# Matmuls of constants into a spare PSUM bank, issued by TensorE behind seven norms of a two-block transformer kernel

## Chip, core and metric

The kernel runs on one core of a Trainium2 chip. The metric is the device time of one launch in microseconds (us); lower is better. Before the change the median of 3 runs is 2633.58 us (2631.14 to 2635.16).

## What is computed

A sequence of 512 tokens of width 1024, all in fp32, goes through two blocks of two layers each. The first block has an mLSTM layer and a forgetting-attention layer, each followed by a gated feed-forward of width 2816 with a short convolution. The second has a layer of spatial gating and neighbourhood attention, a conformer convolution layer, and a feed-forward of width 4096 after each. The part that matters here is the norm, which stands between all the large products:

```python
def rmsnorm(x, w):
    xf = x.astype(jnp.float32)
    y = xf * lax.rsqrt(jnp.mean(xf * xf, axis=-1, keepdims=True) + EPS)
    return (y * w.astype(jnp.float32)).astype(x.dtype)

for layer in range(DEPTH):
    h = rmsnorm(x, norm_mix_pre[layer])
    y = ...
    x = x + rmsnorm(y, norm_mix_post[layer])
    h = rmsnorm(x, norm_ffn_pre[layer])
    y = conv_ffn(h, ...)
    x = x + rmsnorm(y, norm_ffn_post[layer])
```

The second block adds modulated norms of the same kind (`mlp0`, `odd`, `mlp1` below), a layer norm inside the conformer convolution (`conf`), and a last `rmsnorm_2(x, final_g)` (`final`) before the output.

## The kernel before

Activations lie with the features on the 128 partitions: `X`, `Y`, `H_hi`, `H_lo` and `hid_hi`, `hid_lo` are 8 tiles of 128 features by 512 tokens. A large product is computed as three products in a rounded fp32 format (`F32R`): each weight and each activation is split into a high and a low part, and TensorE (PE) multiplies high by high, low by high and high by low. So one product of a 128-row step is three matmuls of 512 columns (line 2277), and one group of 256 output features is 8 steps by 2 halves by 3, 48 matmuls, into a pair of banks of the PSUM tensor `G`. Stages of a few groups follow each other in the order of `linear_plan`.

ScalarE (ACT) makes the high part of each weight chunk (`split_hi`, line 497), VectorE (DVE) the low part (`split_lo`, line 502), SyncE (SP) issues the weight loads, GpSimd (POOL) loads the modulation weights. Every engine's program is written out by hand, in order; semaphores join them. Nothing reorders the work.

A norm goes like this. ACT squares 512-column tiles into `SQ` or `SA`. PE sums the squares over the features by multiplying with the 128x128 tile `ones`, in plain fp32, into bank `M[:, 0]`. ACT takes logarithm and exponential of the sum (lines 435 and 437), which gives the inverse root for each token, in `root` (the profile calls it `Dg`). DVE multiplies it in, and ACT and DVE split the result into `H_hi` and `H_lo`. Only then can PE start the next product. There are three patterns around the change:

- `post0` and `post1` (behind the stages `m_out` and `x_out`): after the sum, DVE adds the normed `Y` to `X` (lines 484 and 479), ACT squares the new `X` (line 445), and PE sums these squares tile by tile (`norm_tiles`, line 2345), in between the matmuls of the next stage (`ffn1`), one sum and six matmuls for each tile.
- `mlp0`, `odd`, `mlp1`: after the sum, DVE and ACT fill `H_hi` and `H_lo` (lines 470, 353, 365), and PE starts the next stage when the first `H_lo` tile is there. `conf` is the same with a SiLU in between (lines 2126, 2015, 2034, 2121).
- `final`: DVE writes the normed tiles to `S` (line 2140), PE transposes them (line 1971), ACT copies them out of PSUM (line 2029), and SP stores them (line 1480).

For all but `conf` the sum is issued by `squares_behind`, one matmul of `ones` with the collected squares `SA` (line 2324) and two with `SQ` (line 2327), behind the last group of a stage. For `conf` it is `norm("conf")`, eight sums (line 2345). A plain fp32 matmul stands in the profile as two weight loads and two matmuls. Bank `M[:, 2]`, the tile `ident` (a 128x128 identity) and the tile `VT` (all small vectors, turned) are there already; `M[:, 2]` holds nothing that is still to be read at the seven places.

Of the kernel before, what the change touches and what calls it, by code (L numbers as in the profile page):

```python
# [33 lines left out]
GC = 256  # L34
# [94 lines left out]
def build(nc, a, out, consts):  # L129

    plan, chunks = linear_plan()
    with ExitStack() as ctx:
# [3 lines left out]
        def at(name, offset, shape, dt=F32):  # L136
            return nc.alloc_sbuf_tensor_at(name, shape, dt, offset=origin + offset)
# [18 lines left out]
        VT = at("VT", 184 * K + 512, [P, VBLOCKS * P])  # L156
# [7 lines left out]
        def small(name, shape, dt=F32):  # L164
            n = 4
            for s in shape[1:]:
                n *= s
            t = at(name, o[0], shape, dt)
            o[0] += -(-n // 32) * 32
            return t  # L170

        ident = small("ident", [P, P])
# [78 lines left out]
        M = ctx.enter_context(nc.psum_tensor("M", [P, 4, 512], F32))  # L251
# [71 lines left out]
        def group_of(name, g):  # L323
            return plan[name]["group"] + g

        def wait_read(eng, name, g):
            n = group_of(name, g)
            eng.wait_ge(pair_read[n % 2], n // 2 + 1)
# [5 lines left out]

        first_use = lambda name, g: group_of(name, g) // 2
        used_after = lambda name: 4 + 2 * group_of(name, plan[name]["groups"])

        ident4 = ident[:].unsqueeze(1).to_broadcast([P, TB, P])

# [374 lines left out]
        def mod_sums(pe, layer):  # L714

            pe.wait_ge(mod_used, 48 * layer + 48)
            for r in range(3 if layer else 4):
                if r == 3:
                    pe.wait_ge(mod_e, 1)
                for c in range(4):  # L720
                    mm = pe.matmul(M[32 * c:32 * c + 32, 1 + r % 3, :], ones[:, 0:32], mod_source(r)[:, c * T:c * T + T],
                                   start=True, stop=True, skip_group_check=True)
                mm.then_inc(mod_p, 1)
# [7 lines left out]
        def mod_columns(pe, layer):  # L731

            count = 3 if layer else 4
            pe.wait_ge(mod_e, 4 * layer + count)
            for r in range(count):
                for q in range(4):
                    first = 16 * r + q
                    mm = pe.matmul(M[:, 3, first:first + 13:4], mod_source(r)[:, q * P:q * P + P], ident[:, 0:P:32],
                                   start=(r == 0 and q == 0), stop=(r == count - 1 and q == 3), skip_group_check=True)
            mm.then_inc(mod_s, 1)  # L740
# [742 lines left out]
        def bias_rows_pe(pe):  # L1483
            pe.wait_ge(rp_dma, 64)
            pe.transpose(M[:, 2, 0:120], rp[:], ident[0:120, 0:120]).then_inc(tb_t, 1)

        def bias_pe(pe):

            pe.wait_ge(tb_r, 8)
            wait_all_read(pe, "c_v")  # L1490
            for u in range(10):
                if u % 2 == 0:
                    pe.wait_ge(sel_dma[u // 2 % 2], 16 * (u // 4 + 1))
                if u >= 4:
                    pe.wait_ge(tb_e, u - 3)
                for c in range(8):
                    for a in range(2):
                        mm = pe.matmul(G[HP * a:HP * a + HP, u % 4, HP * c:HP * c + HP],
                                       sel[:, u // 2 % 2, HP * (8 * (u % 2) + c):HP * (8 * (u % 2) + c) + HP],
                                       rm[:, a, :, :].rearrange("p h r -> p (h r)"), start=(c == 0), stop=(c == 7),  # L1500
                                       skip_group_check=True)
                mm.then_inc(tb_b, 1)
# [409 lines left out]
        def second_pe(pe, linear, linear_units, norm, from_h, squares_behind):  # L1912
            linear("c_k", H_hi, H_lo, need=from_h("ctx"), n=CTX)
            bias_rows_pe(pe)
            linear("c_v", H_hi, H_lo, "T", need=from_h("ctx"), n=CTX)
            norm("even")
            bias_pe(pe)
            pe.wait_ge(tb_e, 10)
            near_pe(pe, linear, linear_units, from_h, squares_behind)

            def ffn2(layer, then):
                for part in range(4):
                    base = HIDDEN[f"s{layer}"] + 4 * part
                    linear(f"s{layer}_up{part}", H_hi, H_lo, need=from_h(f"mlp{layer}"))
                    down = linear_units(f"s{layer}_down{part}", hid_hi, hid_lo,
                                        need=lambda t, base=base: pe.wait_ge(hid_l, base + t // 2 + 2),
                                        behind=squares_behind(then) if part == 3 else None)
                    if layer == 0 and part == 3:
                        mod_sums(pe, 1)
                        next(down)  # L1930
                        next(down)
                        mod_columns(pe, 1)
                    finish(down)

            ffn2(0, "odd")

            def taps(g, p):

                if g == 1:
                    pe.wait_ge(mod_ok, 4)  # L1940
                pe.wait_ge(cv_w, 2 * g + 2)
                wait_read(pe, "p_1", g)
                pe.wait_ge(cv_x, 2 * g + 4)
                pe.wait_ge(cv_d, g + 1)
                low, high = slice(0, HP), slice(HP, P)
                for j in range(HALF_TAPS):
                    here, there = V_TAPS + j, V_TAPS + HALF_TAPS + j
                    for hs, bank in ((low, 2 * p), (high, 2 * p + 1)):
                        pe.matmul(M[hs, bank, :], tap_diag[hs, p, j, :], yp[hs, p, here:here + T], start=(j == 0),
                                  stop=(j == HALF_TAPS - 1), skip_group_check=True)  # L1950
                    for hs, other, bank in ((low, high, 2 * p), (high, low, 2 * p + 1)):
                        mm = pe.matmul(M[other, bank, :], tap_diag[hs, p, HALF_TAPS + j, :],
                                       yp_turned[hs, p, there:there + T], start=(j == 0), stop=(j == HALF_TAPS - 1),
                                       skip_group_check=True)
                mm.then_inc(cv_pe, 1)

            linear("p_1", H_hi, H_lo, need=from_h("odd"), behind=taps)
            wait_read(pe, "p_1", DT - 2)
            for t in range(DT):
                pe.wait_ge(cv_d, t + 3)  # L1960
                mm = pe.matmul(G[:, 0, :], ones[:], Y[:, t, :], start=(t == 0), stop=(t == 7))
            mm.then_inc(cv_s, 1)
            norm("conf")
            linear("p_2", H_hi, H_lo, need=from_h("conf"), behind=squares_behind("mlp1"))
            ffn2(1, "final")
            for t in range(DT):
                pe.wait_ge(fin_t, t + 1)
                if t >= 4:
                    pe.wait_ge(fin_c, t - 3)
                for b in range(TB):  # L1970
                    mm = pe.transpose(G[:, t % 4, b * P:b * P + P], S[:, t % 4, b * P:b * P + P], ident[:])
                mm.then_inc(fin_m, 1)
# [279 lines left out]
        def _(pe):  # L2252
# [62 lines left out]
            def squares_behind(name):  # L2315

                first = 8 * NORM[name]

                def behind(g, p):
                    if g < 3:  # L2320
                        return
                    pe.wait_ge(n_ss, first + 6)
                    pe.wait_ge(n_sd, NORM[name])
                    pe.matmul(M[:, 0, :], ones[:], SA[:, 0, :], start=True, stop=False, skip_group_check=True)
                    for m in range(2):
                        pe.wait_ge(n_sq, first + 7 + m)
                        pe.matmul(M[:, 0, :], ones[:], SQ[:, m, :], start=False, stop=(m == 1),  # L2327
                                  skip_group_check=True).then_inc(n_ss, 1)
                return behind

            def norm(name, blocks=TB, between=None):
# [110 lines left out]
            for t in range(DT):  # L2442
                gate_rows(1, 16, t)
            fox_pe(pe, linear, linear_units, from_h, squares_behind)
            ffn1(1)
            second_pe(pe, linear, linear_units, norm, from_h, squares_behind)

        @block.scalar
# [152 lines left out]
def finish(steps):  # L2601
    for _ in steps:
        pass
# [66 lines left out]
```

## Time and profile before

| | before |
|---|---|
| median of 3 runs | 2633.58 us (2631.14 to 2635.16) |
| profiled execution: span from the first to the last instruction | 2636.9 us |
| PE busy, share of the span | 2533.4 us, 96% |
| PE weight loads | 2006.7 us, 76% |
| DVE busy | 1537.5 us, 58% |
| ACT busy | 1027.1 us, 39% |
| mean granted clock of PE | 0.981 |
| share of PE in the chain that ended last | 86% |

The profiled execution is a single one and has no time of its own beside its span; the three runs are 1.7 to 5.8 us shorter than that span. The granted clock is a share of 2.4 GHz: 1.00 is 2.4 GHz, and 0.50 is 1.2 GHz; a mean between them is a stretch with some of each. The chain is the work that ended last, followed back from step to step. PE's matmuls are pipelined, so the ends in the profile lie a little behind the time at which the next matmul can start.

### The profile page before, as it was taken

Reading aid. Unit: us, or ns where it says so; the run is one execution under the profiler, and the core shown is the slowest. Engines: PE = TensorE matmul, PEld = TensorE weight load, DVE = VectorE, ACT = ScalarE, POOL = GpSimd, SP = SyncE. Lnnn points to the kernel's source line nnn. Section 1 sums busy time; section 2 is a strip of 40 time slices with the busy share of each in tenths; the row PEclk is TensorE's granted clock in tenths of the full one; section 3 lists DMA queues with packets and bytes.
Section 4 is the critical chain, followed back from the end, with each engine's and each line's share of the span. In section 5 each row is a group of like instructions: output and inputs, shape, how many; then the busy total and the mean of one; then the engine's idle time right before and its main releaser. Section 6 shows DMA issues by size and latency. Waiting matters only on the chain.

```text
span 2636.9 us, 31348 instructions
## 1 busy us (share of the span) xinstructions
PE 2533.4 (96%) x12464; PEld 2006.7 (76%) x12464; DVE 1537.5 (58%) x2568; ACT 1027.1 (39%) x1581; POOL 96.2 (4%) x133
## 2 busy tenths in 40 slices
PE   7999999999999989999998998999999998999998
PEld 6887788887776667888876875788888665788887
DVE  6455676867455656646565256666653897534433
ACT  4344543424435555434245235323223324422323
POOL 0000001010000000000000000011100110000000
PEclk9999999999999999999999999999999999999999
DMA  5322335464221122333324220366652221233331
GB/s 171 112 81 80 88 97 171 147 177 134 66 88 49 55 69 77 96 96 96 92 74 136 72 73 17 116 196 193 191 158 88 64 65 33 87 96 96 96 98 54
DMA packets 285080, 266.86 MB, mean 101 GB/s; under 512 B 13331, under 2 KB 270663, under 8 KB 284935
## 3 DMA queue, kind: packets, MB, share of 16 engines
q1 hardware_dynamic: 268503, 210.33, 26.0%
q0 software_dynamic: 15024, 54.33, 7.0%
q8 instruction: 99, 1.62, 0.3%
q10 hardware_dynamic: 1408, 0.20, 0.0%
q14 instruction: 46, 0.38, 0.0%
HBM read 262.72 MB, written 2.10 MB: 100 GB/s over the span
## 4 chain that ended last, share of the span: by engine, by line
PE 86%; DVE 8%; ACT 3%; issue 2%; SPq 1%; DMA 0%; POOL 0%; ACTq 0%; DVEq 0%; POOLq 0%
PE G L2277 70%; PE G L2293 7%; DVE Y L2097 2%; PE M L2345 1%; DVE S L2097 1%; DVE w_lo L502 1%; PE M L1143 1%; PE M L798 1%; PE M L808 1%; PE M L2327 1%; PE M L1618 1%; PE M L1154 1%; PE M L1165 1%; PE M L1607 0%; ACT w_hi L497 0%
## 5 line engine op out<-in xcount | busy, mean ns | idle before, releaser
L502 DVE TENSOR_TENSOR w_lo<-raw,w_hi 128x1024 fp32r<-128x1024 f32 x396 | 482.8, 1224 | 675.2 <-ACT w_hi L497 674.3
L2277 PE MATMUL G<-H_hi,w_hi 128*128 128x512 f32 (+1 forms) x2016 | 808.4, 401 | 20.2 <-DVE H_lo L365 12.0
L2277 PE MATMUL G<-H_lo,w_hi 128*128 128x512 f32 (+1 forms) x2016 | 788.5, 391 | 0.0
L2277 PE MATMUL G<-H_hi,w_lo 128*128 128x512 f32 (+1 forms) x2016 | 788.4, 391 | 0.0
L497 ACT ACTIVATE w_hi<-raw 128x1024 fp32r<-128x1024 f32 x396 | 417.2, 1056 | 935.8 <-PE G L2277 828.4
L2277 PEld LDWEIGHTS G<-H_hi,w_hi 128*128 128x128 f32 x2016 | 383.5, 190 | 127.3 <-issue 46.1
L2277 PEld LDWEIGHTS G<-H_hi,w_lo 128*128 128x128 f32 x2016 | 382.9, 190 | 80.6
L2277 PEld LDWEIGHTS G<-H_lo,w_hi 128*128 128x128 f32 x2016 | 383.5, 190 | 79.4 <-issue 4.7
L2277 PE MATMUL G<-hid_hi,w_hi 128*128 128x512 f32 x864 | 339.4, 393 | 7.5 <-DVE hid_lo L621 4.7
L2277 PE MATMUL G<-hid_lo,w_hi 128*128 128x512 f32 x864 | 338.5, 392 | 0.0
L2277 PE MATMUL G<-hid_hi,w_lo 128*128 128x512 f32 x864 | 338.5, 392 | 0.0
L2277 PEld LDWEIGHTS G<-hid_hi,w_hi 128*128 128x128 f32 x864 | 163.6, 189 | 43.5 <-DVE hid_lo L621 5.5
L2277 PEld LDWEIGHTS G<-hid_hi,w_lo 128*128 128x128 f32 x864 | 163.7, 189 | 34.4
L2277 PEld LDWEIGHTS G<-hid_lo,w_hi 128*128 128x128 f32 x864 | 163.7, 189 | 34.0
L2293 PE MATMUL G<-w_hi,H_hi 128*128 128x256 f32 x480 | 140.3, 292 | 1.5 <-DVE H_lo L453 1.4
L600 DVE SCALAR_TENSOR_TENSOR S<-SQ,VT,S 128x511 f32<-128x511 f32 (+1 forms) x176 | 128.2, 750 | 19.4 <-ACT S L562 16.2
L2293 PE MATMUL G<-w_hi,H_lo 128*128 128x256 f32 x480 | 136.8, 285 | 0.0
L2293 PE MATMUL G<-w_lo,H_hi 128*128 128x256 f32 x480 | 136.7, 285 | 0.0
L682 DVE SCALAR_TENSOR_TENSOR mod_acc<-mod_w,cs,mod_acc 128x512 f32<-128x512 f32 x168 | 125.9, 749 | 3.4
L660 POOL DMA_DIRECT2D mod_w<-in_w_mod x96 | 69.5, 724 | 1067.0 <-DVE mod_acc L682 476.5
L2293 PEld LDWEIGHTS G<-w_hi,H_hi 128*128 128x128 f32 x480 | 93.0, 194 | 13.0 <-issue 6.4
L562 ACT ACTIVATE S<-SQ,VT 128x512 f32<-128x512 f32 x88 | 67.0, 809 | 88.2 <-DVE SQ L607 88.2
(329 smaller groups left out, 2390.4 us busy)
## 6 DMA issues: line engine op xcount, KB each, us to landing
raw<-in_w_ff SPq DMA_DIRECT2D x128, 512.0 KB
mod_w<-in_w_mod POOLq DMA_DIRECT2D x96, 512.0 KB, 4.5
raw<-in_ffn_w_up SPq DMA_DIRECT2D x176, 256.0 KB
raw<-in_ffn_w_down SPq DMA_DIRECT2D x40, 512.0 KB
raw<-in_w_in SPq DMA_DIRECT2D x28, 512.0 KB
raw<-in_mlstm_w_in SPq DMA_DIRECT2D x24, 512.0 KB
raw<-in_kv_w SPq DMA_DIRECT2D x16, 512.0 KB
raw<-in_fox_w_qg SPq DMA_DIRECT2D x16, 512.0 KB
```

The costliest lines, as they stand in the source:

```text
L497: act.activation(w_hi[:, j, :], raw[:, j, :], ACT.Copy).then_inc(hi_done, 1)
L502: dve.tensor_tensor(w_lo[:, j, :], raw[:, j, :], w_hi[:, j, :], ALU.subtract).then_inc(lo_done, 1)
L562: act.activation(S[:, h, :], SQ[:, h, :], ACT.Identity, bias=VT[:, ds(t + cb, 1)], scale=VT[:, ds(t + (cw + 88), 1)]).then_inc(f_a, 1)
L600: return dve.scalar_tensor_tensor(S[:, h, k:T], SQ[:, h, 0:T - k], w, S[:, h, k:T], ALU.mult, ALU.add)
L660: pool.dma_start(mod_w[:, n % 2], src[:, 2 * quarter:2 * quarter + 2, block * 512:block * 512 + 512]).then_inc(mod_landed[n % 2], 16)
L682: one = dve.scalar_tensor_tensor(acc[:, cols], w, c, acc[:, cols], ALU.mult, ALU.add)
L798: return pe.matmul(M[:, bank, col:col + T - s * P], mK[hs, h // 2, s * P:s * P + P], mQ[hs, h // 2, s * P:T], start=(col == 0), stop=True, ...
L808: mm = pe.matmul(M[:, 2 + b // 2, (b % 2) * (P + 1):(b % 2 + 1) * (P + 1)], m_part(h, s)[:, (b - s) * P:(b - s) * P + P], mV[:, s, h, :], ...
L1143: mm = pe.matmul(M[:, e, 0:(b + 1) * P], xQ[hs, q, b * P:b * P + P], xK[hs, q, 0:(b + 1) * P], start=True, stop=True)
L2097: link.post(dve.scalar_tensor_tensor(acc, yp[:, p:p + 1, j:j + T], tap(j), acc, ALU.mult, ALU.add))
L2277: mm = pe.matmul(G[:, 2 * p + m, 0:n], lw[:, k, ms], rh[:, t, 0:n], start=(t == 0 and q == 0), stop=(t == st["ktiles"] - 1 and q == 2), sk ...
L2293: mm = pe.matmul(G[:, 2 * p + b // 2, (b % 2) * GC:(b % 2) * GC + GC], lh[:, t, bs], rw[:, k, :], start=(t == 0 and q == 0 and b % 2 == 0) ...
```

## The change

A helper of the build function issues a number of matmuls that multiply the first 256 columns of `VT` by `ident` and write to bank `M[:, 2]`. They wait for no semaphore and raise none, and nothing reads their result. It is called at the end of `squares_behind` (so behind the sums of `post0`, `post1`, `mlp0`, `odd`, `mlp1` and `final`; `fpost0` and `fpost1` pass there too, with no entry in the table) and behind `norm("conf")`. It is 54 matmuls in all.

```diff
+        WARM = {"post0": 8, "post1": 8, "mlp0": 8, "odd": 8, "mlp1": 8, "final": 4, "conf": 10}
+
+        def keep_warm(pe, name):
+
+            for _ in range(WARM.get(name, 0)):
+                pe.matmul(M[:, 2, 0:GC], ident[:], VT[:, 0:GC], start=True, stop=True, skip_group_check=True)
+
...
             mm.then_inc(cv_s, 1)
             norm("conf")
+            keep_warm(pe, "conf")
             linear("p_2", H_hi, H_lo, need=from_h("conf"), behind=squares_behind("mlp1"))
...
                         pe.matmul(M[:, 0, :], ones[:], SQ[:, m, :], start=False, stop=(m == 1),
                                   skip_group_check=True).then_inc(n_ss, 1)
+                    keep_warm(pe, name)
                 return behind
```

On PE, at `post0`, the program before has the three sums and then the first sum of the next norm (the first name behind the arrow is what streams, the second what is loaded as weights):

```order
L2277 MATMUL G<-H_hi,w_lo 128x512
L2324 MATMUL M<-S,ones 128x512
L2327 MATMUL M<-SQ,ones 128x512 x2
L2345 MATMUL M<-SQ,ones 128x512
L2277 MATMUL G<-H_hi,w_hi 128x512
```

In the changed program, whose lines are numbered a little higher, the same place reads:

```order
L2285 MATMUL G<-H_hi,w_lo 128x512
L2332 MATMUL M<-S,ones 128x512
L2335 MATMUL M<-SQ,ones 128x512 x2
L343 MATMUL M<-VT,ident 128x256 x8
L2354 MATMUL M<-SQ,ones 128x512
L2285 MATMUL G<-H_hi,w_hi 128x512
```

The eight matmuls stand between the last sum of the one norm and the first sum of the next; no other instruction has moved.

## Rows read from the trace of the kernel before

**Rows 1.** The page: span, busy time of the engines, the chain's shares

```profile
span 2636.9 us, 31348 instructions
...
PE 2533.4 (96%) x12464; PEld 2006.7 (76%) x12464; DVE 1537.5 (58%) x2568; ACT 1027.1 (39%) x1581; POOL 96.2 (4%) x133
...
PE 86%; DVE 8%; ACT 3%; issue 2%; SPq 1%; DMA 0%; POOL 0%; ACTq 0%; DVEq 0%; POOLq 0%
```

**Rows 2.** Waits of PE: waited for, us in total, times, longest

```profile
PE G L2277 <- DVE H_lo L365: 12.0, 3, 4.1
...
PE M L2345 <- ACT SQ L445: 9.5, 3, 4.4
...
PE G L2277 <- DVE H_lo L2121: 5.4, 1, 5.4
...
PE G L1971 <- DVE S L2140: 2.2, 1, 2.2
```

**Rows 3.** Windows: us, busy by engine (instructions), granted clock, DMA

```profile
284.00:292.00 8.00, 5.50 (x11) 3.30 (x11) 7.96 (x13) 3.73 (x6) 0.00 (x0) 0.57 0.00 0
...
2626.00:2630.00 4.00, 3.79 (x19) 3.80 (x20) 4.00 (x7) 1.92 (x4) 0.00 (x0) 0.57 0.06 20
```

**Rows 4.** Timeline of PE and DVE behind the sum of `mlp1`

```profile
2271.22 0.71 PE L2277 MATMUL G<-H_hi,w_hi 128*128 128x512 f32 x1 [3.94 <-DVE H_lo L365]
2271.65 0.75 DVE L365 SCALAR_TENSOR_TENSOR H_lo<-S,mod,H_hi 128x512 fp32r<-128x512 f32 x1
2271.72 0.63 PE L2277 MATMUL G<-H_lo,w_hi 128*128 128x512 f32 x1
...
2272.15 0.63 PE L2277 MATMUL G<-H_hi,w_lo 128*128 128x512 f32 x1
...
2272.97 0.75 DVE L365 SCALAR_TENSOR_TENSOR H_lo<-S,mod,H_hi 128x512 fp32r<-128x512 f32 x1
...
2274.94 0.40 PE L2277 MATMUL G<-H_hi,w_hi 128*128 128x512 f32 x1
```

**Rows 5.** Chain that ended last: start, us, what; around six of the norms

```profile
286.50 2.05 PE M L2345 x2
...
293.63 0.86 PE M L2345 x2
...
1007.54 1.25 PE M L2345 x2
...
1012.63 1.38 PE G L2277 x6
...
1302.04 0.86 PE M L2345 x4
1302.90 10.93 PE G L2277 x48
...
1690.47 9.58 PE G L2277 x34
...
2054.59 13.56 PE G L2277 x48
...
2218.38 46.17 PE G L2277 x192
```

**Rows 6.** Timeline of ACT at the start of stage `p_1`

```profile
2068.23 1.06 ACT L497 ACTIVATE w_hi<-raw 128x1024 fp32r<-128x1024 f32 x1 [3.16 <-PE G L2277]
```

**Rows 7.** Timeline of DVE and ACT at the end of the program

```profile
2625.40 5.39 DVE L2140 SCALAR_TENSOR_TENSOR S<-X,VT,Dg 128x512 f32<-128x512 f32 x8 [3.35 <-ACT Dg L437]
...
2629.87 2.56 ACT L2029 ACTIVATE x_tm<-G 128x512 f32<-128x512 f32 x5 [0.23 <-PE G L1971]
```

**Rows 8.** Windows, columns as in rows 3: only fp32 sums; short waits; a fall elsewhere

```profile
2205.50:2213.00 7.50, 7.46 (x16) 2.22 (x15) 6.39 (x14) 4.08 (x7) 0.00 (x0) 1.00 0.00 0
...
2188.00:2206.00 18.00, 15.14 (x82) 5.64 (x75) 16.68 (x27) 3.77 (x5) 0.00 (x0) 1.00 0.18 57
629.00:637.00 8.00, 5.66 (x18) 4.19 (x18) 5.56 (x8) 4.03 (x4) 0.72 (x1) 0.79 0.12 38
```

## The prediction, made before the changed kernel was run

> **What bounds the kernel now.** I read the page first. PE is busy 2533.4 of 2636.9 us and has 86% of the chain that ended last [rows 1]: time is won by making PE wait less or run faster, and nearly nothing else. So I read PE's waits. At the norms of the change PE stands still seven times: three times for the first `H_lo` of `mlp0`, `odd` and `mlp1`, 12.0 us together; for line 445 at `post0` and `post1`, 4.4 us each (a third, short wait of that line is at another norm); 5.4 us at `conf`; 2.2 us before the last transposes [rows 2]. These 28 us are a chain through ACT and DVE that nothing shortens here.
>
> Next the granted clock. Behind `post0` it is 0.57 over 8 us, which is (1 - 0.57) / 0.5 x 8 = 6.9 us at the lower level, 1.2 GHz; behind `final` 3.4 us [rows 3]. All seven places have such a spell, 34 us by the same working. Before each PE had stood idle; while it lasts PE is at work again. At `mlp1` matmuls of 512 columns start 0.43 us apart (2271.72, 2272.15) [rows 4]; at full clock it is 10.93 / 48 = 0.228 [rows 5]. The question is how much of the low time is PE at work on the chain.
>
> **The change part by part.** *The added work.* A plain fp32 matmul of 256 columns is two passes; four passes took 0.86 us, 0.215 us each (the x4 row of [rows 5]). Eight matmuls are 16 passes, 3.4 us; ten are 4.3; four are 1.7. They start as soon as the last sum has been fed in. The waits are 4.4, 4.4, 3.9, 4.1, 3.9 (8 matmuls each), 5.4 (10) and 2.2 us (4) [rows 2, 4]. So at 2.4 GHz each batch ends 0.5 to 1.1 us before PE is needed, and costs nothing. The sums' own semaphore is raised before the batch, so ACT is not held up; the batch has no waits, no loads from memory, and its bank is read by nobody. ACT, DVE, POOL and the DMA queues get no instruction. If a batch ran at 1.2 GHz throughout it would take 6.9 us and reach 3 us into the work behind it.
>
> *The waits.* They stay what they are: the ends of the ACT and DVE chain do not move.
>
> *The work behind each wait, at 2.4 GHz.* I price each from the chain [rows 5], against stretches at full clock: 48 matmuls 10.93 us (0.228 each), a 512-column sum 0.86, six matmuls 1.38.
>
> - `post0`: from 286.50 to 293.63 PE does two sums and twice six matmuls, 7.13 us. At full clock: 1.25 for the first sum and its wait for `H_lo` (as at `post1`), 1.38, 0.86, 1.38, together 4.87. Gain 2.3.
> - `post1`: the same stretch, 1007.54 to 1014.01, is 6.5 us. Gain 1.6.
> - `mlp0`: 34 matmuls took 9.58 us against 34 x 0.228 = 7.7. That is 1.85, less 0.15: the first matmul out of a wait runs through empty pipelines, and the row takes that in (a matmul lasts 0.40 at full clock, where the next starts 0.23 behind it [rows 4]). Gain 1.7.
> - `odd`: 48 took 13.56 against 10.93; less 0.15. Gain 2.5.
> - `conf`: 192 took 46.17 against 43.7; less 0.15. Gain 2.3.
> - `mlp1`: 9 starts from 2271.22 to 2274.94, 3.72 us against 9 x 0.228 = 2.05 [rows 4]. Gain 1.7.
> - `final`: DVE hands over its last tile at 2625.40 + 5.39 = 2630.79. The 19 transposes in 3.79 us [rows 3] are 0.2 each, most of them at the lower level, so the four of a tile are some 0.4 at full clock; ACT starts 0.23 behind them and takes 2.56 / 5 = 0.5 to 0.6. It would end near 2632.1 instead of 2629.87 + 2.56 = 2632.43 [rows 7]. Gain 0.3: DVE sets the pace next, and the low clock there was nearly hidden.
>
> The sum is 12.4 us. Two checks on it. PE at full clock needs a tile each 6 x 0.228 = 1.37 us, and DVE delivers `H_lo` each 1.32 us (2271.65, 2272.97) [rows 4]: the supply is just quick enough, with 0.05 us to spare, so no new stall; were it 0.15 us slower, the seven tiles behind the first would cost each of four places some 0.7. Behind `odd` follows a stage that DVE bounds, but its first step waited 3.16 us on PE [rows 6], so the 2.5 us pass on. The stages behind the others are long runs of PE's own matmuls.
>
> *Does the clock stay up?* This is the one term that the trace doesn't hold. Bounds: nothing (the batches don't act on the clock), and the full 12.4; for a loss see the last rival. For the full value: over 7.5 us in which PE ran nothing but plain fp32 sums, with one operand constant, the clock stayed at 1.00; over 18 us with 2.9 us of idle in pieces, and with many matmuls whose weights are diagonal (`tap_diag`), it stayed at 1.00 too [rows 8]. Behind the batches 0.5 to 1.1 us of idle are left. The shortest single waits that I found a fall behind were 2.2 us (`final`) and 2.3 (629 to 637, 8.00 less 5.66 busy) [rows 2, 8]. I take the full value, as the nearest rows are on that side.
>
> The Trainium skill ("TensorE: Matmul & The Clock Gate", "Part 4: PE-mode transpose") says that the full clock doesn't engage for transposes. A product with an identity is close to one, and by that rule the sum would be 0 instead of 12.4. But at `final` PE ran nothing but transposes after its wait, and the clock was low for 3.4 us and high again before 2630 [rows 3]: the row contradicts the rule, and a batch is an ordinary matmul besides.
>
> My sum is made against the profiled execution, which spans 2636.9 us and has no other time; it would become 2624.5. The median of the runs is 3.3 us below that span, so the prediction is 2633.6 - 12.4 = 2621.2 us. About 0.2%, 5.3 us, is what can be told from no change.
>
> **The rivals.**
>
> *The batches don't hold the clock* (12%). The falls come as late as before, so they catch the last passes of a batch at most, and the slack of 0.5 to 1.1 us takes most of that. Time as before, 2633.6. For it: the operands are constants, one of them an identity, and no row has just that; against it: the sums and the diagonal weights of [rows 8]. This is what the skill's rule on transposes would bring, and the row at `final` speaks against it.
>
> *Held at some places only* (9%). Where the rest of the idle time (1.1 us at `conf`, 0.9 at `post0` and `post1`, each with a further short wait behind the first sum) still brings a fall, the place gives nothing. Half of the gain: 2627.4.
>
> *The batches reach into the work* (5%, slower). Every pass loads its weights anew, and a load takes 2006.7 / 12464 = 0.16 us in the mean [rows 1]. If load and pass didn't overlap, a pass would cost 0.16 + 0.215 = 0.375, eight matmuls 6.0 us, ten 7.5, four 3.0. PE would be late by 1.6, 1.6, 2.1, 1.9, 2.1, 2.1 and 0.8, together 12.2 us. It decides from 3.9 / 16 = 0.245 us a pass. With the clock held the two cancel; if the stop and go doesn't hold it, the time is 2645.8. Against it: the 256-column passes of the x4 row overlapped, at 0.215 [rows 5]. The skill's same page ("What overlaps and what doesn't") says that a load overlaps a running matmul only in another row group, which would make every pass serial; that row contradicts it, since its loads and passes all use the same 128 rows.
>
> **How the numbers follow.** Held everywhere has 74%, and a spread of some 4 us to either side, from the supply by DVE (up to 3 us lost) and from the runs themselves (4 us between the lowest and highest of three): 2617 to 2625. With the partial case up to 2629 the range holds 83%; what is left out is the unchanged case and the slower one. Faster by over 0.2%: 0.74 + 0.09 = 0.83; the same: 0.12; slower: 0.05.
>
> **What would show it.** Seven groups of 256-column matmuls on line 343, passes 0.21 to 0.22 us apart. PE's waits of line 2277 on line 365 fall from 12.0 to about 2, that on 2121 from 5.4 to about 1. The clock is 1.00 in the 8 us behind each norm, and the mean rises from 0.981 to about 0.987 (100 us of low clock less 34). The 48 matmuls at `odd` take about 11.0 us. The other low spells, some 65 us, stay. I am wrong if the clock still falls at the seven places, if matmuls behind a batch start later after the norm's exponential than before, or if the saved time turns up as PE waiting on DVE inside the first group.

## The result, and the profile after

| | before | after |
|---|---|---|
| median of 5 runs | 2634.83 us (2631.14 to 2636.44) | 2616.83 us (2613.73 to 2619.77) |
| ratio to before, with its 95% interval | | 0.9928 [0.9916, 0.9940] |
| profiled execution: time | 2638.7 us (its span and the 1.8 us that lie around it in after) | 2616.83 us |
| profiled execution: span, mean granted clock | 2636.9 us, 0.981 | 2615.0 us, 0.991 |

The change takes 18.0 us off the median, where I had forecast 12.4. The sign was right, and so was the mechanism at the seven places; the size was a third too small, and the median lies just below my range.

The page, span, busy times and the chain's shares, to set beside [rows 1]:

```profile
span 2615.0 us, 31564 instructions
...
PE 2538.2 (97%) x12572; PEld 2010.9 (77%) x12572; DVE 1536.5 (59%) x2568; ACT 1027.7 (39%) x1581; POOL 98.0 (4%) x133
...
PE 85%; DVE 8%; ACT 3%; issue 3%; SPq 1%; DMA 0%; POOL 0%; ACTq 0%; DVEq 0%; POOLq 0%
```

PE has 108 matmul rows more, two for each of 54 added matmuls. They took some 23 us (54 x 2 x 0.215), yet PE's busy time grew by 4.8 only. Everything else on PE became some 18 us shorter.

PE's waits, to set beside [rows 2] (line numbers are 7 to 9 higher now: 365 is 372, 445 is 452, 2121 is 2129, 2140 is 2148):

```profile
PE M L2354 <- ACT SQ L452: 2.7, 3, 1.1
...
PE G L2285 <- DVE H_lo L372: 1.6, 3, 0.6
...
PE G L2285 <- DVE H_lo L2129: 1.1, 1, 1.1
...
PE G L1979 <- DVE S L2148: 0.5, 1, 0.5
```

12.0 us became 1.6, 9.5 became 2.7, 5.4 became 1.1, 2.2 became 0.5. Nothing is gained by that in itself, since the batches fill what was idle. Three batches with the work behind them, from PE's timeline (at `post0`, `mlp1` and `final`):

```profile
283.16 3.62 PE L343 MATMUL M<-VT,ident 128*128 128x256 f32 x16
...
287.68 1.10 PE L2354 MATMUL M<-SQ,ones 128*128 128x512 f32 x2 [0.90 <-ACT SQ L452]
```

```profile
2247.53 3.62 PE L343 MATMUL M<-VT,ident 128*128 128x256 f32 x16
2251.63 0.47 PE L2285 MATMUL G<-H_hi,w_hi 128*128 128x512 f32 x1 [0.49 <-DVE H_lo L372]
...
2253.56 0.40 PE L2285 MATMUL G<-H_hi,w_lo 128*128 128x512 f32 x1
```

```profile
2602.64 1.89 PE L343 MATMUL M<-VT,ident 128*128 128x256 f32 x8
```

Sixteen passes take 3.62 us, with the tail of the last; the seven batches end 0.5 to 1.1 us before PE is wanted (1.1 at `conf`), as worked out. Behind `mlp1` nine matmuls start within 1.93 us (2251.63 to 2253.56), where they took 3.72 [rows 4].

Windows over two of the places, to set beside [rows 3], and the chain's pieces that answer to [rows 5] (`odd`, `conf`):

```profile
284.00:292.00 8.00, 7.00 (x27) 4.64 (x27) 7.21 (x12) 4.41 (x8) 0.00 (x0) 1.00 0.05 20
...
2602.50:2606.50 4.00, 3.49 (x18) 2.32 (x17) 2.28 (x4) 2.03 (x4) 0.00 (x0) 1.00 0.02 4
```

```profile
2038.28 11.16 PE G L2285 x48
```

```profile
2201.17 43.80 PE G L2285 x192
```

The clock is 1.00 where it was 0.57. 48 matmuls at `odd` take 11.16 us instead of 13.56, 192 at `conf` 43.80 instead of 46.17.

**Where the rest came from.** I laid the two traces beside each other by DVE's instructions, which are the same 2568 in the same order, and read how far the second is ahead. The seven places account for 12.0 of the 21.9 us between the two profiled executions. The other 9.9 lie where no instruction was changed. Windows of equal content (the same matmuls by their count), of before and then of after, at the stage behind `kv` (from 620 on), in the attention part of the second layer (from 1340 on), and at 2000:

```profile
620.00:720.00 100.00, 94.87 (x548) 77.62 (x547) 56.09 (x76) 43.71 (x69) 2.17 (x3) 0.95 0.30 93
1340.00:1520.00 180.00, 160.53 (x1093) 134.17 (x1092) 85.29 (x134) 77.23 (x114) 5.77 (x11) 0.93 0.32 99
...
2000.00:2016.00 16.00, 16.00 (x77) 13.47 (x76) 3.23 (x5) 5.74 (x7) 0.00 (x0) 0.89 0.21 67
```

```profile
619.20:715.30 96.10, 90.20 (x548) 73.41 (x547) 55.89 (x76) 43.42 (x69) 2.17 (x3) 1.00 0.32 97
1334.80:1507.00 172.20, 155.23 (x1093) 130.56 (x1092) 85.17 (x134) 77.09 (x114) 5.77 (x11) 0.97 0.34 103
...
1985.30:1999.80 14.50, 14.50 (x77) 12.39 (x76) 3.21 (x5) 5.85 (x7) 0.00 (x0) 1.00 0.24 72
```

The same 548, 1093 and 77 matmuls take 3.9, 7.8 and 1.5 us less, and of the columns only the granted clock differs much. (0.9 of the 3.9 is lost again near 935, 1.4 are lost ahead of `post0`, and 1.1 at a new fall, which lies at 2187 in after.) So spells of low clock went away that have no added batch near them. Is that the change's doing, or does any execution have its own?

### The profile page after: what moved, and what is told of

Its sections match the earlier page's. It is cut to its first block, busy times and chain, and to the rows that moved or that the text cites. A ratio compares the mean times of both kernels' runs of the same rounds, so it can differ in the third digit from the quotient of the medians.

```text
span 2615.0 us, 31564 instructions
## 1 busy us (share of the span) xinstructions
PE 2538.2 (97%) x12572; PEld 2010.9 (77%) x12572; DVE 1536.5 (59%) x2568; ACT 1027.7 (39%) x1581; POOL 98.0 (4%) x133
## 4 chain that ended last, share of the span: by engine, by line
PE 85%; DVE 8%; ACT 3%; issue 3%; SPq 1%; DMA 0%; POOL 0%; ACTq 0%; DVEq 0%; POOLq 0%
PE G L2285 69%; PE G L2301 7%; DVE Y L2105 2%; PE M L2354 1%; DVE S L2105 1%; DVE w_lo L509 1%; PE M L1150 1%; PE M L805 1%; PE M L815 1%; PE M L1625 1%; PE M L1161 1%; PE M L2335 1%; PE M L1172 1%; PE M L1614 0%; ACT w_hi L504 0%
```

## The experiments

All kernels below compute the whole output. The low time of an execution is (1 - its mean granted clock) x 2 x its span, as in the prediction; a mean over the runs of a kernel is good to some 1 to 4 us. The first four shared a chip, and so did each four that follow.

### The change itself, and its parts

`whole` is the change unchanged. `few` asks whether the batches have to fill the wait; `post` and `fill` are parts.

```diff
-        WARM = {"post0": 8, "post1": 8, "mlp0": 8, "odd": 8, "mlp1": 8, "final": 4, "conf": 10}
+few:    WARM = {"post0": 1, "post1": 1, "mlp0": 1, "odd": 1, "mlp1": 1, "final": 1, "conf": 1}
+post:   WARM = {"post0": 8, "post1": 8}
+fill:   WARM = {"mlp0": 8, "odd": 8, "mlp1": 8}
```

> The changed kernel once more, unaltered. Its first comparison gave a ratio of 0.9928 (0.9916 to 0.9940), 18 us less, where the seven places of the profile add up to 12.4. Theory A (chance): low-clock spells away from the seven places fall differently in every execution, and five runs of each kernel happened to differ by some 5 us in favour of the change. Then a second set of runs comes out nearer to 12 to 14 us, a ratio of 0.9947 to 0.9953. Theory B (something systematic away from the seven places, such as waits of TensorE on VectorE that shrink): again 17 to 19 us, a ratio of 0.9928 to 0.9936, and the profile shows the same short wait on line 643 (1.2 us, 2.8 before) and no low clock behind line 738's successor again.

> One matmul (two passes, 0.43 us) at each of the seven places, so 3.1 to 5.0 us of idle are left. If the gain comes through the clock, as predicted, the clock falls as before at post0, post1, mlp0, odd, mlp1 and conf; the time is that of before, within 0.1 to 0.2% (0 to 3 us less). If it comes from anything else that a matmul ahead of the stage does (weight loads that start sooner, TensorE's own queue), most of the 18 us stay.

> Batches at post0 and post1 alone. By the prediction's terms 2.3 + 1.6 = 3.9 us less; the place post1 alone spent only 3.4 us at the low clock in the profile of before and post0 spent 6.9, and if the mean over executions lies between these, each is worth about 2.2 and the sum 4.4. Theory B would give more than 6 us. The profile shows no low clock in the 8 us behind either sum, and low spells behind mlp0, odd, conf and mlp1 as before.

> Batches at mlp0, odd and mlp1 alone. By the prediction's terms 1.7 + 2.5 + 1.7 = 5.9 us less, by a mean over executions 6.5. Theory B would give more than 8 us. In the profile the 48 matmuls at odd take about 11.0 us instead of 13.6.

Measured, against 2635.41 us before (median of 21 runs on that chip, mean low time 95 us):

| kernel | median us (range, runs) | ratio [95%] | mean low time, us |
|---|---|---|---|
| `whole` | 2617.18 (2615.22 to 2621.03, 5) | 0.9931 [0.9917, 0.9945] | 49 |
| `post` | 2625.81 (2619.27 to 2628.71, 5) | 0.9964 [0.9951, 0.9977] | 69 |
| `fill` | 2629.00 (2622.11 to 2631.68, 11) | 0.9975 [0.9967, 0.9984] | 80 |
| `few` | 2634.76 (2630.92 to 2639.06, 11) | 0.9998 [0.9989, 1.0007] | 92 |

`few` is no faster: one matmul at each place leaves most of the wait, and the clock falls at five of the seven places (at `odd`, with 3.7 us of stall left, and at `final`, with 1.8, its profiled execution has no fall). Its waits and its window at `post0`:

```profile
PE G L2285 <- DVE H_lo L372: 10.7, 3, 3.7
PE M L2354 <- ACT SQ L452: 8.6, 3, 3.9
```

```profile
284.00:292.00 8.00, 4.08 (x10) 2.10 (x9) 6.01 (x10) 4.49 (x8) 0.00 (x0) 0.70 0.16 60
```

So it is the filling of the wait that works, not the presence of line 343. `whole` gives 18 us again, so the size is no accident of one go. `post`, whose two terms are 3.9 us, gives 9.6; the low time falls by 26 us, where its two places held 10. `fill`, with 5.9 us of terms, gives 6.4, and its low time falls by 16 us, where its places held 14.

### What one place gives

`post0`, `post1` and `conf` keep one entry of the table each. `transposes` keeps all and replaces the operation:

```diff
-                pe.matmul(M[:, 2, 0:GC], ident[:], VT[:, 0:GC], start=True, stop=True, skip_group_check=True)
+                for part in range(4):
+                    pe.transpose(M[:, 2, 0:P], VT[:, 0:P], ident[:])
```

> Batch at post0 alone. Both at post gave 9.6 us where the terms say 3.9. Theory C: the low spells start on a beat of their own, and where they fall against the program is fixed by the last spell before them. In the profiles of before, few and fill the spells between 284 and 1430 us are the same ones at the same places (285, 633, 691, 937, 1008, 1370, 1394), two of them where TensorE is not idle long or at all; in post and after most of them are gone or half as long. Then post0 alone takes its own 2.3 us and, in most executions, some 3 to 5 us at the spells up to 1008: 4 to 7 us less, and the profile lacks the low spell at 691 or has others between 285 and 1008 than before. Theory D: each place is worth its own term and the 9.6 us were chance: 2.2 us less (1 to 3.5), and the spells at 633, 691 and 937 stand as before.

> Batch at post1 alone. Theory C: the spells up to 937 are those of before, at 285, 633, 691 and 937, and behind 1008 the ones at 1370 and 1394 (6.8 us each) change or shorten in the profile; 4 to 7 us less in all. Theory D: 1.6 to 2.2 us less, with 1370 and 1394 as before.

> Batch at conf alone. Both theories: 2.3 us less (1 to 4), 192 matmuls of p_2 in 43.8 us instead of 46.2; if the terms of post, fill and conf are added, 9.6 + 6.4 + 2.3 + 0.3 for final = 18.6, against 18.2 measured for all.

Against 2633.20 us before (27 runs, mean low time 92 us):

| kernel | median us (range, runs) | ratio [95%] | mean low time, us | its own term |
|---|---|---|---|---|
| `post0` | 2632.62 (2624.41 to 2635.25, 11) | 0.9997 [0.9988, 1.0006] | 87 | 2.3 |
| `post1` | 2628.97 (2627.74 to 2633.40, 11) | 0.9989 [0.9980, 0.9998] | 82 | 1.6 |
| `conf` | 2632.90 (2629.70 to 2636.19, 11) | 0.9998 [0.9989, 1.0007] | 93 | 2.3 |
| `transposes` | 2619.99 (2615.83 to 2621.24, 5) | 0.9950 [0.9937, 0.9964] | 58 | 12.4 |

The single places are at the edge of what can be told. `post0` and `conf` alone give about nothing, and both miss what I expected of them (4 to 7 us by theory C, or 2.2, for `post0`; 2.3 for `conf`), though their intervals, up to 3.2 and 2.9 us of gain, hold the terms. In the profile of `post0` the fall at `post0` is gone and those at 633, 691 and 937 stand. In that of `conf` the fall at `conf` is gone, and there is a spell of 6.8 us at `mlp1`, 50 us on, where before has 3.4. Over all its runs `conf` has no less low time than the kernel before (93 us against 92), though its place held 6.8: what is taken away at one place can come back elsewhere. `post1` gives more than its term, and its profile shows where: in the attention part, 350 us behind the batch, the same 1093 matmuls as above run almost at full clock.

```profile
1339.60:1510.10 170.50, 152.00 (x1093) 128.49 (x1092) 84.99 (x134) 77.24 (x114) 5.77 (x11) 0.99 0.33 104
```

That is 9.5 us less than the 180.00 before, and nearly all of the 9.8 us between the two profiled executions. The runs as a whole show 3 to 4 us less, so most of the 9.5 is the spread between executions: the profiled one of before had its worst there (24 us of low time; in the six other profiles without a batch at `post1` it was 10 to 20).

Transposes hold the clock at all seven places too. More on them below.

### A shift, a second go, a longer batch, more places

`shift` is the kernel before with four of these matmuls at a place where PE never waits, so that all that follows moves 1.7 us later. `post_again` is `post`. `double` has batches twice as long. `more` adds batches at further waits that ACT or DVE ends.

```diff
+shift:   if part == 1 and layer == 0:
+shift:       for _ in range(4):
+shift:           pe.matmul(M[:, 2, 0:GC], ident[:], VT[:, 0:GC], start=True, stop=True, skip_group_check=True)
         linear(f"f{layer}_up{part}", H_hi, H_lo, need=need,
...
+double:  WARM = {"post0": 16, "post1": 16, "mlp0": 16, "odd": 16, "mlp1": 16, "final": 8, "conf": 20}
...
+more:    WARM.update({"fpost0_mid": 3, "fpost1_mid": 8, "down2": 4, "even_first": 4, "gating": 5})
```

> The kernel before, with no batch at any norm, but four matmuls of the same kind put into dense work of TensorE, ahead of stage f0_up1 (about 400 us into the span). They are 1.7 us of added work on the path and stand behind no wait. Theory C (the low spells start on a beat of their own, and the spell at post0 fixes where the next ones fall): the spells at 633, 691 and 937 are hit at another point of the beat and shorten or vanish in the profile, so the time is 1 to 6 us less than that of before plus 1.7: between 2629 and 2634 where before is 2634. Theory D (spells elsewhere are chance): spells as in before, and 1.7 us more.

> Batches at post0 and post1, unaltered from the run named post. Its five runs gave a mean of 10.1 us less; post0 alone gave 1.6 and post1 alone 3.7, and the terms say 3.9. Theory C: again 7 to 12 us less, and the low spells outside the seven places come to 35 to 50 us in the profile instead of 61 to 68. Theory D: 4 to 5 us less.

> All seven batches twice as long: 16, 20 and 8 matmuls. By the price of 0.215 us a pass a batch takes 6.9, 8.6 and 3.4 us and reaches 2.5, 2.5, 3.0, 2.8, 3.0, 3.2 and 1.2 us beyond the waits of before, 18.2 us together. The clock stays up as in the changed kernel, so the time is its 2617 + 18 = 2635. If passes did not overlap with their weight loads it would be 2617 + 50 or more.

> The changed kernel with batches in five more waits of TensorE: 3 and 8 matmuls between the first and second sum at fpost0 and fpost1 (waits 1.4 and 3.5 us), 4 ahead of the last hidden tile in stages f0_down2 and f1_down2 (2.3 us), 4 ahead of the sums of norm even (2.2 us), 5 ahead of the product with Dg in the gating (2.6 us). In the profile of the changed kernel the spells there are those at 1354, 1388 and 1415, 3.4 us each, and the waits at 629 and 1486 had none. I expect 3 to 6 us less than the changed kernel: 2611 to 2614, with no low spell behind these five waits. If the spells only move to other places, the time stays at 2617.

Against 2633.70 us before (29 runs, mean low time 93 us):

| kernel | median us (range, runs) | ratio [95%] | mean low time, us |
|---|---|---|---|
| `shift` | 2633.82 (2626.07 to 2638.02, 12) | 0.9999 [0.9991, 1.0007] | 86 |
| `post_again` | 2627.29 (2624.13 to 2631.32, 11) | 0.9976 [0.9967, 0.9985] | 71 |
| `double` | 2633.75 (2630.55 to 2638.47, 10) | 1.0001 [0.9992, 1.0009] | 52 |
| `more` | 2620.80 (2617.65 to 2624.51, 5) | 0.9954 [0.9942, 0.9966] | 53 |

`double` is the cleanest result of the study: it has the low clock of the change (52 us against 49) and the time of before. At `post0` a batch of 32 passes ends when PE was long wanted, and no wait is left behind it:

```profile
284.23 7.07 PE L343 MATMUL M<-VT,ident 128*128 128x256 f32 x32
291.13 1.02 PE L2354 MATMUL M<-SQ,ones 128*128 128x512 f32 x2
```

It gives away the whole 18 us that the change brings, so the length of a batch is as hard a limit as the fall on the other side.

`post_again` gives 6.3 us: more than the terms, less than the 7 to 12 that I had expected.

`shift` should have cost 1.7 us of added work and cost nothing measurable; but its interval reaches to a loss of 1.8 us, so the time alone decides nothing. Its low time is 86 us where before has 93, which is clear of the error of such means, though not by much. Its profile, one execution, has no low clock from 620 to 720, though nothing was added or taken away there but time, and more at `post1` than before:

```profile
682.00:700.00 18.00, 18.00 (x134) 15.75 (x133) 6.20 (x13) 9.39 (x16) 0.00 (x0) 1.00 0.33 92
1004.00:1012.00 8.00, 3.85 (x7) 2.41 (x8) 6.74 (x11) 4.88 (x8) 0.00 (x0) 0.67 0.00 0
```

`more` is not better than the change but gives less, 12 us against 18. I had forecast 3 to 6 us more. The five waits that it fills are 1.4 to 3.5 us long, and its clock doesn't fall at the filled waits, yet its low time is not below the change's. One place in its profile stands out. Near 1430 PE waits for two loads of `sel`, which land after 5.3 and 5.0 us, where in the 17 other profiles they take 3.7 to 4.7, and 10.2 us of low clock lie around these waits. The row of `more`, and that of after:

```profile
PE G L1507 <- DMA sel<-const_sel: 7.2, 2, 3.8
```

```profile
PE G L1505 <- DMA sel<-const_sel: 4.4, 3, 2.3
```

This stretch alone is 6.9 us longer than in after, of the 7.7 between the two spans. Whether the batches ahead of it bring that about or this one execution (the slowest of its five runs) had it by chance, no run separates.

### The halves on one chip

The parts had run on other chips than the whole. Open was whether the excess over 12.4 us comes from an interaction between the places. `rest` is the complement of `post`; the other three repeat kernels above.

```diff
-        WARM = {"post0": 8, "post1": 8, "mlp0": 8, "odd": 8, "mlp1": 8, "final": 4, "conf": 10}
+rest:   WARM = {"mlp0": 8, "odd": 8, "mlp1": 8, "final": 4, "conf": 10}
```

> The change unchanged, beside its two halves on one chip. Theory E (the halves act on each other: with the early falls gone, more of the later ones stay away): 2616 to 2618 us, some 17.5 below the kernel before, and 3 us or more beyond what the two halves give together. Theory F (the terms add up, and the 5 us beyond my sum are spread between goes): 2619 to 2622 us, the two halves' gains added, within 2.

> Batches at post0 and post1 alone, a third go. By the terms 3.9 us less than before; the two goes so far gave 9.7 and 6.4. Theory E: 6 to 9 less again, since what these two batches remove lies mostly behind them. Theory F: between 4 and 7.

> The other five batches alone (mlp0, odd, mlp1, final, conf). By the terms 8.5 us less than before. Theory E: 8 to 9, the terms alone, so that with the other half's 6 to 9 the sum stays 1 to 3 under the whole. Theory F: the whole's gain less the other half's.

> Each matmul of a batch as four transposes, beside the change on the same chip. If transposes do as well as matmuls: within 2 us of it. If the 3 us between 2620.0 and 2617.2 in the earlier goes was the operation and not the chip: 3 us above it again.

Against 2633.82 us before (15 runs, mean low time 96 us; one run of `whole_b` at 5132 us is outside every other and left out):

| kernel | median us (range, runs) | ratio [95%] | mean low time, us | its terms |
|---|---|---|---|---|
| `whole_b` | 2615.33 (2613.97 to 2615.94, 4) | 0.9931 [0.9917, 0.9944] | 46 | 12.4 |
| `post_b` | 2627.25 (2623.15 to 2629.87, 11) | 0.9974 [0.9966, 0.9983] | 75 | 3.9 |
| `rest` | 2626.45 (2621.75 to 2627.21, 5) | 0.9967 [0.9955, 0.9980] | 70 | 8.5 |
| `transposes_b` | 2619.36 (2617.86 to 2622.67, 5) | 0.9949 [0.9935, 0.9962] | 55 | 12.4 |

The gains, from the ratios and the chip's 2633.8 us: 18.2 [14.7, 21.9] for the whole, 6.8 [4.5, 9.0] for `post_b`, 8.7 [5.3, 11.9] for `rest`. The halves add up to 15.5, 2.7 short of the whole, and that gap is within the intervals. So both theories are hurt: the whole is well below the 2619 to 2622 that plain addition by my terms had, but an interaction of 3 us or more between the halves isn't shown either.

What is shown is that the first half exceeds its terms. `rest` gives what its five terms say (8.7 for 8.5), if within a wide interval. The pair `post0` and `post1` gave 9.5, 6.3 and 6.8 us in three goes for terms of 3.9, and 3.9 is below the interval in each, barely in the second (4.0 to 8.7). The low time tells the same without the clock's price: `rest` takes away 26 us, where its places hold 24 in the trace of before; `post` took away 26, 22 and 21, where its places hold 10. These two come first in the program, so their surplus can only lie behind them. Alone, `post0` took away 5 us of low time (its place held 6.8) and `post1` 10 (its place 3.4): of the two, `post1` shows a surplus by itself. By windows of `rest` and `whole_b` over the same stretches:

```profile
1339.90:1513.40 173.50, 156.28 (x1093) 130.92 (x1092) 85.22 (x134) 77.15 (x114) 5.79 (x11) 0.96 0.33 103
620.00:720.00 100.00, 94.87 (x547) 77.63 (x546) 56.05 (x76) 43.65 (x68) 2.17 (x3) 0.95 0.31 93
```

```profile
1333.40:1505.60 172.20, 155.10 (x1093) 130.40 (x1092) 85.07 (x134) 77.24 (x114) 5.79 (x11) 0.97 0.34 103
```

`rest` leaves 620 to 720 as it was before. That much is bound to be: all its batches lie behind both stretches. For the same reason its 173.50 in the attention part, 6.5 us below the 180.00 of before, is spread between executions, and the window pair by itself shows only 1.3 us. So I listed the low time of both stretches in all 18 profiles. The stretch from 620 to 720 lies behind `post0` and ahead of `post1`, so only a batch at `post0` can act on it:

| profiles | low time from 620 to 720 |
|---|---|
| 7 without a batch at `post0` (before, `few`, `fill`, `conf`, `post1`, `shift`, `rest`) | 10.2 in six, 0 in `shift` |
| 11 with one | 10.2 in four (`whole`, `post0`, `post_again`, `double`), 6.8 in two (`transposes`, `more`), 0 in five |

| profiles | low time from 1340 to 1520 |
|---|---|
| 7 without a batch at `post1` (before, `few`, `fill`, `conf`, `post0`, `shift`, `rest`) | 24, 17, 20, 14, 14, 10, 14: mean 16 |
| 11 with one (after, `whole`, `post`, `post1`, `transposes`, `post_again`, `double`, `more`, `whole_b`, `post_b`, `transposes_b`) | 10, 14, 10, 3, 7, 3, 3, 14, 10, 10, 10: mean 9 |

The first table leans towards an effect and can't prove one. In the second the means are 7 us apart, with an error of some 2 (estimated from the spread of the values), and ten of the eleven have the batch at `post0` too.

Less, not gone: the profiled execution of `whole` has the 10.2 us from 620 to 720, and that of `whole_b`, with the same code, has none.

## Why the prediction was right, and where it was wrong

**The added work: right.** 0.215 us a pass was to hold, and does (16 passes in 3.62 us, the last one's tail included). The batches cost nothing beside the waits, which `double` confirms from the other side. Against the kernel before on its own chip it gains nothing (0.0 us by the medians), where `whole` gains 18.2; the excess of its batches over the waits, worked out by the same pass price, is 18.2.

**The clock holds: right.** This was the term that the trace did not contain. In 15 profiles a place is filled by a full batch or one of transposes (after and all kernels but `few` and `shift`), and none of them has low clock at a filled place. That `few` gains nothing shows that it isn't enough to have a matmul ahead of the stage. The rivals (clock falls all the same; held at some places; batches reach into the work) are all out. The last would have needed 0.245 us a pass. The margin was thinner than I had read, though: I gave 2.2 us as the shortest stall with a fall behind it, and in the trace of before the fall at 223.3 stands behind stalls of at most 1.6 us, and the one at 1605.7 behind stalls of at most 1.8 (both in stretches with several). The batches leave 0.5 to 1.1.

**The seven terms: right, to within 0.3 each.** In the profile of after against [rows 3 to 5, 7]:

| place | forecast | measured | from |
|---|---|---|---|
| `post0` | 2.3 | 2.0 | first sum to third, 7.13 to 5.10 (287.68 to 292.78) |
| `post1` | 1.6 | 1.5 | the same, 6.5 to 4.94 (1003.89 to 1008.83) |
| `mlp0` | 1.7 | 1.6 | 43 matmuls 11.62; now 55 in 12.73, less 12 at 0.228, 10.0 |
| `odd` | 2.5 | 2.4 | 48 matmuls |
| `conf` | 2.3 | 2.4 | 192 matmuls |
| `mlp1` | 1.7 | 1.8 | nine starts, 3.72 to 1.93 |
| `final` | 0.3 | 0.3 | DVE's start to ACT's end, 7.03 to 6.73 |
| sum | 12.4 | 12.0 | |

The chain's pieces behind `post0` and `post1`, and the tail on DVE and ACT, which answers to [rows 7]:

```profile
288.88 1.65 PE G L2285 x6
290.53 0.86 PE M L2354 x2
291.39 1.39 PE G L2285 x6
292.78 0.86 PE M L2354 x2
```

```profile
1003.89 1.10 PE M L2354 x2
1004.99 1.60 PE G L2285 x6
...
1008.83 0.86 PE M L2354 x2
```

DVE's supply of `H_lo`, which had 0.05 us to spare, made no new stall, and the 2.5 us of `odd` passed on through the stage behind it: ACT waited 3.16 us there [rows 6], and now

```profile
2049.53 1.06 ACT L504 ACTIVATE w_hi<-raw 128x1024 fp32r<-128x1024 f32 x1 [0.76 <-PE G L2285]
```

**The failed step: "The other low spells, some 65 us, stay."** They don't. Low time went from 95 or 96 us in the mean to 49 (`whole`) and 46 (`whole_b`), 46 to 50 us less, of which the seven places had 34. That the 34 is no accident of one trace the other profiles tell: in ten of them (before, `shift`, and the kernels with full batches at some of the places only), each place holds, while it has no batch, a mean that adds up to 33.7 us over the seven. So 12 to 16 us of low clock went away elsewhere. The price of low clock at the seven places is 12.4 / 34.1 = 0.36 us for each us; by it the missing spells are worth 4 to 6 us, and that is the 5.6 between 18.0 and 12.4. The kernels bear this price out as wholes: `whole`, `post`, `post_again`, `post_b` and `rest` gain 0.3 to 0.4 us of median for each us of low time that they lose. The mean clock shows it too: 0.991 where I wrote 0.987. I had priced the places as if the spells elsewhere were fixed to their own causes, and had checked this in one trace only. The step fails the other way too: `conf` alone loses the fall at its place and no low time in sum.

A second, smaller flaw in the same step: I took the low time of one execution as the kernel's. Its 99 us and its 24 in the attention part were high (the mean is 92 to 96). My sum stood at that span less 12.4 and I then moved it to the median; I did not ask how much the spells of unchanged stretches vary, which the spread of the three runs (4 us) had hinted at.

**How the batches remove spells elsewhere is only half settled.** Shown: the first two batches together (`post0` and `post1`) give more than their terms, in three goes; the profiles with them have less low clock some 350 us behind them, in the mean; nothing there was changed. In its one profile, a mere shift of 1.7 us changes those spells as well. My reading is that a fall needs a gap and also the right moment, and that an earlier spell, by delaying the program or by fixing the moment, decides which later gaps are caught. The two windows below fit that, but no run isolates it, and the falls with PE busy throughout, below, don't fit. Not settled is whether the halves add up, and why `more` gains less.

## What to carry to other kernels

Where a matmul-bound kernel stalls PE for 2 to 5 us on a chain through other engines, matmuls of constants into a free bank keep the clock up and cost nothing, if they end before PE is wanted; a batch twice as long gave everything back. Price each place from low-clock and full-clock rows of the same instructions, but then ask what low clock the rest of the kernel has, since it may move too, and read its spread over executions before using one trace's value. Count low time in every run, from its granted clock: here it told a batch that doesn't hold the clock (`few`) from one that holds it and is too long (`double`), at equal times.

## What was unexpected in the hardware

**The same gap has a fall behind it in one execution and none in another.** Before and after have the same stall of 2.3 us near 629 (5.66 us busy of 8): the clock there was 0.79 [rows 8] and is 1.00 now. Near 1356 it is the other way round, in these windows of before and of after:

```profile
1354.00:1362.00 8.00, 5.66 (x25) 4.35 (x25) 5.39 (x10) 4.41 (x8) 0.00 (x0) 1.00 0.01 3
```

```profile
1348.80:1356.80 8.00, 5.67 (x19) 4.26 (x19) 5.39 (x10) 4.41 (x8) 0.00 (x0) 0.83 0.00 1
...
627.00:635.00 8.00, 5.66 (x26) 4.33 (x25) 5.52 (x9) 4.67 (x5) 0.00 (x0) 1.00 0.06 21
```

**The clock falls with PE busy throughout.** Before, line 738 issues 16 matmuls of four columns, 32 passes, from 688.20 on:

```profile
688.20 2.74 PE L738 MATMUL M<-ident,mod_acc 128*128 128x4 f32 x24
690.79 1.75 PE L738 MATMUL M<-ident,ctx_acc 128*128 128x4 f32 x8
```

As the profile counts it, PE is busy in all of the 8 us around them, with no wait ahead, and the clock was 0.68; it falls at 690.9, behind 2.7 us of these short passes. In after it is 1.00 there, with the same code. It is not the only one: in the window from 2000 to 2016 of before, shown further up, PE is busy for 16.00 of 16.00 us, 24 such passes of line 738 stand in it, and the clock falls at 2008.5; in after there is no fall. Of the 18 profiles 12 have the first of these falls and 13 the second. The windows of before and of after:

```profile
688.00:696.00 8.00, 8.00 (x52) 8.00 (x52) 2.63 (x4) 2.00 (x2) 0.00 (x0) 0.68 0.70 198
```

```profile
686.40:694.40 8.00, 8.00 (x71) 7.85 (x71) 3.34 (x9) 2.58 (x4) 0.00 (x0) 1.00 0.72 199
```

**Transposes hold the clock, a little less well.** `transposes_b` has 1.00 at all seven places; these are `post0` and `final`:

```profile
284.00:292.00 8.00, 7.03 (x43) 5.25 (x42) 6.58 (x11) 5.04 (x8) 0.00 (x0) 1.00 0.12 49
...
2602.00:2608.00 6.00, 5.51 (x29) 3.31 (x28) 2.44 (x4) 2.22 (x5) 0.00 (x0) 1.00 0.00 0
```

The Trainium skill ("TensorE: Matmul & The Clock Gate", "Part 4: PE-mode transpose") says that the full clock doesn't engage for transposes. By that `transposes` would be no faster than before; the measured ratios are 0.9950 [0.9937, 0.9964] and 0.9949 [0.9935, 0.9962], so the fp32 transposes of this case contradict it. Beside the change on one chip it is some 4 us slower all the same (every run of `transposes_b` is above every counted run of `whole_b`), with 10 us more low time. That isn't at the seven places; the waits and the length of a batch are alike (3.66 us for 32 passes against 3.62 for 16). Which property of a transpose does that I haven't tried.
